# Delta rule of an RWKV-7 layer on Trainium2: one gram product a head, u and v stacked, a bank of its own for the solving

## What is computed

```
sa = einsum('bhvk,bhk->bhv', S, kk_t)
S  = S * w_t[:, :, None, :] - sa[..., None] * b_t[:, :, None, :] + v_t[..., None] * k_t[:, :, None, :]
y_t = einsum('bhvk,bhk->bhv', S, r_t)
```

## Time and profile before

| what | value |
| --- | --- |
| median of 3 runs | 1472.24 us (1471.99 to 1473.29) |
| the profiled execution | 1476.32 us, of which the profile's span is 1474.5 us |
| mean granted PE clock | 0.972 |
| PE busy | 1351.4 us of the span (92%) |
| DVE busy | 783.9 us (53%) |
| ACT busy, POOL busy | 578.9 us (39%), 224.0 us (15%) |
| DMA | 178.46 MB in 249079 packets, of which 151343 are under 512 B |

### The profile page before, as it was taken

How to read it: one execution, slowest core, us unless ns; L and a number is a source line. 1 busy time by engine, 2 the same in 40 slices (tenths; PEclk the granted TensorE clock), 3 DMA queues, 4 the chain that set the end, 5 groups by cost and what they waited for, 6 DMA issues and landing times. The chain is left out here.

```text
span 1474.5 us, 37647 instructions
## 1 busy us (share of the span) xinstructions
PE 1351.4 (92%) x16154; PEld 1215.1 (82%) x16154; DVE 783.9 (53%) x1588; ACT 578.9 (39%) x1178; POOL 224.0 (15%) x335
## 2 busy tenths in 40 slices
PE   7999999999999888777878869999999999998997
PEld 6989898887899887776777748899999997665785
DVE  6737245777831257867777754561111122776545
ACT  6726246876831022222222242441111132876324
POOL 0000000000000255545544700000001000214000
PEclk9999999999999689999999989999999999999998
DMA  5724122567595344455446345024334236431202
GB/s 206 225 60 100 63 89 90 150 180 233 167 262 171 81 95 95 101 116 132 110 99 137 82 163 217 29 84 147 95 91 120 63 110 180 149 102 35 88 29 93
DMA packets 249079, 178.46 MB, mean 121 GB/s; under 512 B 151343, under 2 KB 220911, under 8 KB 247999
## 3 DMA queue, kind: packets, MB, share of 16 engines
q1 hardware_dynamic: 216951, 161.10, 38.5%
q10 hardware_dynamic: 31968, 15.04, 3.6%
HBM read 115.95 MB, written 60.46 MB: 120 GB/s over the span
## 5 line engine op out<-in xcount | busy, mean ns | idle before, releaser
L369 PE MATMUL mix_acc<-mix_high,mix_w_high 128*128 128x364 f32 (+1 forms) x768 | 177.8, 340 | 11.2 <-ACT mix_high L435 10.0
L369 PE MATMUL mix_acc<-mix_low,mix_w_high 128*128 128x364 f32 (+1 forms) x768 | 172.0, 332 | 1.2 <-DVE mix_low L589 1.2
L369 PE MATMUL mix_acc<-mix_high,mix_w_low 128*128 128x364 f32 (+1 forms) x768 | 170.9, 331 | 0.0
L369 PEld LDWEIGHTS mix_acc<-mix_high,mix_w_high 128*128 128x128 f32 x768 | 130.1, 189 | 30.3 <-issue 28.5
L369 PEld LDWEIGHTS mix_acc<-mix_low,mix_w_high 128*128 128x128 f32 x768 | 132.9, 189 | 2.3 <-DVE mix_low L589 2.1
L369 PEld LDWEIGHTS mix_acc<-mix_high,mix_w_low 128*128 128x128 f32 x768 | 133.5, 189 | 0.2 <-DVE mix_w_low L603 0.2
L1579 PE MATMUL out_acc<-qkvg_room_r_high,qkvg_room_w_high 128*128 128x364 f32 (+1 forms) x320 | 105.8, 331 | 1.0 <-DVE qkvg_room_w_low L1931 1.0
L603 DVE TENSOR_TENSOR mix_w_low<-mix_wt,mix_w_high 128x1024 fp32r<-128x1024 f32 x32 | 39.2, 1224 | 124.9 <-ACT mix_w_high L441 124.5
L1579 PE MATMUL out_acc<-qkvg_room_r_low,qkvg_room_w_high 128*128 128x364 f32 (+1 forms) x320 | 105.1, 329 | 0.0
L1579 PE MATMUL out_acc<-qkvg_room_r_high,qkvg_room_w_low 128*128 128x364 f32 (+1 forms) x320 | 105.1, 328 | 0.0
L1929 DVE CAST qkvg_room_w_high<-qkvg_room_wt 128x1024 fp32r<-128x1024 f32 x20 | 14.2, 710 | 155.4 <-DMA qkvg_room_wt<-in_w_att 155.4
(11 more groups left out here) (284 smaller groups left out, 3220.5 us busy)
## 6 DMA issues: line engine op xcount, KB each, us to landing
mix_wt<-in_w_in SPq DMA_DIRECT2D x32, 512.0 KB, 4.6
qkvg_room_wt<-in_w_att SPq DMA_DIRECT2D x20, 512.0 KB, 3.8
delta_bk<-scr_bk SPq DMA_DIRECT2D x17, 512.0 KB, 4.8
delta_kr<-scr_kr SPq DMA_DIRECT2D x17, 512.0 KB, 7.8
scr_kr<-mix_outs SPq DMA_DIRECT2D x16, 512.0 KB, 3.9
scr_bk<-mix_outs SPq DMA_DIRECT2D x16, 512.0 KB, 4.7
early_xpad<-in_xpad SPq DMA_DIRECT2D x8, 548.5 KB, 8.6
scr_xg<-early_xs SPq DMA_DIRECT2D x8, 544.0 KB, 3.0
```

The source lines that it names most:

```text
L369: mm = pe.matmul(acc[:, s, k, 0:width], w[:, s, d, :], r[:, d, n0:n0 + width], start=d == 0 and q == 0, stop=d == DT - 1 and q == 2)
```

## The change

- **Grams**: `bk` is stored as (pair, side, 64), with the two sides exchanged for head 1. One product of a head takes both sides as 128 columns of weights: rows of 64, columns of 128. Bank `gram`p now holds head p, with b's gram on the head's own half and k's on the other. The signs of the masks go by head.
- **u and v stacked**: `uv` holds for each pair and head u on the head's own half and v on the other. `end_y` and the state's update (`make_s`) each contract over all 128 partitions in one product of a head, rows of 128 and columns of 64; the value products of y and of the state are gone. `begin_z` still takes v alone. ACT copies u in two halves (`keep_u`).
- **Rows**: `turn_rows` sends head p to bank `gram`p, both sides, each a quarter; there are as many products as before.
- **Banks**: the solving gets a bank of its own, `solve`; both halves of a level's two products share `level0` and `level1`; the state's update and the turned y use `state_out`.
- ACT copies b's gram to a plain tile `lower` (`keep_lower`, two operations of 64 partitions), from which POOL takes the diagonal blocks and the levels' masks.
- **Order**: `make_grams(front, 0)` comes ahead of `make_u(behind)`; y is turned and gated one turn later; `begin_z` runs beside `make_lm(i, 0)`; `spread_blocks` comes ahead of `make_lm(i, 2)`, `end_z` ahead of `grow(i, 2)`. DVE masks the second half of the grams ahead of the centring, and solves columns 0 to 3 ahead of `scale_y`.
- **Transfers**: `bk` comes in four transfers a chunk (one before), v straight into `uv` in pieces of 64 floats (2 KB rows before).

The core of the diff:

```diff
+def load_pair_of_keys(sp, bk, loaded, scr, slot, t, cols):
+    for p, half in enumerate((slice(0, 64), slice(64, 128))):
+        for k in range(2):
+            sp.dma_start(bk[half, slot, :, k ^ p, :], scr["bk"][t, half, k, :, cols]).then_inc(loaded, 16)
...
-                    for p, f in zip(HALVES, FLIPPED):
-                        sp.dma_start(v_rows[f, c % 3], scr["vt"][c, p]).then_inc(v_loaded[c % 3], 16)
+                    for p in range(2):
+                        sp.dma_start(uv[FLIPPED[p], c % 3, :, p, :], scr["vt"][c, HALVES[p]]).then_inc(v_loaded[c % 3], 16)
...
+                        for p, half in enumerate(HALVES):
+                            mm = pe.matmul(gram_bank[p][:, 128 * j:128 * j + 128], bk[half, c % 2, pair].rearrange("p k n -> p (k n)"), kr[half, c % 4, :, pair, :], start=True, stop=True)
...
+                        for p, half in enumerate(HALVES):
+                            unit = end_diag[half, pair, :] if c < SAMPLE else unit64[half, :]
+                            for side, out_half in enumerate(HALVES):
+                                mm = pe.matmul(gram_bank[p][out_half, 64 * pair:64 * pair + 64], bk[half, slot, pair, side, :], unit, start=True, stop=True)
...
+                def make_s(c):
+                    pe.wait_ge(u_kept, 2 * c + 2)
+                    for p in range(2):
+                        pe.wait_ge(rows_kept[p], c + 1)
+                    if c:
+                        pe.wait_ge(y_gated, c)
+                    for pair in range(DT):
+                        for p, half in enumerate(HALVES):
+                            mm = pe.matmul(state_bank[half, 64 * pair:64 * pair + 64], rows[:, c % 2, pair, p, :], uv[:, c % 3, pair, p, :], start=True, stop=True)
...
+                            mm = pe.matmul(wide_bank[half, 64 * pair:64 * pair + 64], grams[:, c % 3, pair, p, 1, :], uv[:, c % 3, pair, p, :],
+                                           start=False, stop=True, skip_group_check=True)
...
+                def keep_lower(c):
+                    for p, half in enumerate(HALVES):
+                        act.wait_ge(gram_kept[p], 2 * c + 2)
+                        act.activation(lower[half], grams[half, c % 3, :, p, 0, :], ACT.Copy).then_inc(lower_kept, 1)
```

More of the change, by code:

```diff
@@ L1072, in _ @@
                         pool.tensor_tensor(s_sample[:, pair], s_sample[:, pair], end, ALU.mult).then_inc(own_ended, 1)
+                    if front < SAMPLE:
+                        mask_level(front, 0)
+                        mask_level(front, 1)
+                    if 0 <= i < SAMPLE:
+                        end_state(i)
+                    if live(i):
+                        shift_bonus(i)
+                    if front == SAMPLE:
+                        pool.wait_ge(v_sample_loaded, 32)
+                        for b in range(NB):
+                            own = seq_mask[:, b:b + 1].rearrange("p (j n) -> p j n", j=1).broadcast_to([128, DT, 64])
+                            pool.tensor_tensor(v_own[:, b], v_sample[:], own, ALU.mult).then_inc(v_owned, 1)
             @block.tensor
@@ L1171, in end_z @@
+                def end_z(c):
+                    if c:
+                        pe.wait_ge(s_kept, c)
+                    else:
+                        pe.wait_ge(zeroed, 3)
                     pe.wait_ge(z_begun, c + 1)
                     for pair in range(DT):
-                        for p in HALVES:
-                            o = chain_bank[p, 64 * pair:64 * pair + 64]
+                        for half in HALVES:
+                            o = chain_bank[half, 64 * pair:64 * pair + 64]
@@ L1282, in _ @@
                     if live(behind):
[L1283 removed]
+                        begin_y(behind)
                         end_y(behind)
[L1285 to L1290 removed]
                     if live(front):
@@ L1295, in _ @@
                     if 0 <= i < SAMPLE:
+                        wait_for_values(i)
+                        make_lm(i, 0, lambda pair: begin_z(i, pair))
+                        grow(i, 0)
+                    if 0 <= behind < SAMPLE:
+                        make_s(behind)
+                    if live(front):
+                        turn_rows(front)
+                    if 0 <= i < SAMPLE:
                         make_lm(i, 1)
@@ L1298, in _ @@
                     if live(front):
-                        turn_rows(front)
+                        spread_blocks(front)
                     if i == -1:
@@ L1557, in _ @@
                     if live(front):
-                        mask_grams(front, 1, 1)
+                        sum_blocks(front)
                     if 0 <= behind < SAMPLE:
@@ L1563, in _ @@
                     if live(front):
-                        sum_blocks(front)
+                        solve_columns(front, range(4))
                     if 0 <= behind < SAMPLE:
@@ L1568, in _ @@
                         add_grown(i, 2)
-                    if 0 <= behind < SAMPLE:
-                        gate_y(behind)
-                    if live(front):
-                        solve_columns(front, range(4))
 def three_passes(pe, out, w_high, w_low, r_high, r_low, columns):
@@ L2515, in constants @@
     seq = tok[:, None] // NT == tok[None, :] // NT
-    gram = np.stack([np.stack([sign * (m & part)[:, 0:64] for sign, m in ((-1.0, before), (-1.0, upto), (1.0, before), (1.0, upto))], 1)
-                     for part in (np.ones_like(seq), seq)], 1)
+    signs = [np.where(head == p, -1.0, 1.0)[:, None] for p in range(2)]
+    gram = np.stack([np.stack([sign * (m & part)[:, 0:64] for sign in signs for m in (before, upto)], 1) for part in (np.ones_like(seq), seq)], 1)
     col = np.arange(64)
```

350 lines of the change are left out of this document (163 added, 187 removed).

## The result

The changed kernel takes 1459.31 us, the median of four runs (1456.65 to 1461.29), beside 1472.76 us (1471.99 to 1473.55, four runs) for the kernel before. The ratio is 0.9897, with a 95% interval of 0.9867 to 0.9928: faster by 13.4 us (10.6 to 19.6 by the interval), where 32 were forecast. The time lies inside the range of 1418 to 1470; the forecast saving is 2.4 times the measured one and lies outside the interval.

What follows compares the result with a forecast made beforehand. PE, held up by late instruction refills and waits, was taken as the bound, with DVE's 16.0 us a turn as floor; 15 x (20.28 - 17.7) = 39, less 7, saves 32 us: 1444 profiled, 1440 median, range 1418 to 1470.

Steps and rivals of the forecast that it cites:

- The gaps: PE pauses inside equal products, read as late instruction refills: 3.3 us a turn, falling to 1.1 with fewer records.
- The rival in which the refills don't ease: Instruction queue bound by other transfers: gaps stay at 2.8 us a turn or more, 1467 us; 15 in 100.
- Side by side and the changes of shape: New product shapes still share the array; nine more shape changes a turn cost 0.1 us each, 0.9 us.
- the slower rival: Gram halves, end_y and make_s not side by side, each 1.95 us for 0.98: 1490 us; 10 in 100.
- the 0.27 end: Upper cost of a shape change on PE, 0.27 us, if a drain hides nothing of the first product; sum 1461.
- waits for ACT and DVE: The other 2.1 us of PE's 20.28 us turn, the mask's 0.6 among them; 0.8 left after the change.
- the part on the new order: Reordering removes the rows' 0.6 us mask wait and hides ACT's copies; new waits at make_lm and make_u.
- edits at nothing: Edits priced at no time: ACT's extra copies (1.8 us at most), SP's extra transfers, v's smaller pieces, POOL's moved queue.
- forecast turn of 17.7 us: Delta-stage turn after the change: 14.9 stages, 0.9 shape changes, 0.8 waits, 1.1 gaps; before, 20.28 us.
- not a matter of the clock: In the delta stage, a granted PE clock of 0.97 taken as upper level nearly all the time; no term given.
- Start and end: Turn 15's late v_own (5 us), last chunk's u copies (1.2) and turn 0's begin_z (1): 7 us lost.
- the last row of the table: Stretch from the copy of z of chunk 16 to the kernel's end: no change forecast, 0 us.

Runs made afterwards that it cites:

- idle_products: The changed kernel plus 48 products a turn in idle quarters of the array, results unread: 1489.9 us, ratio 1.0065 to the kernel before.
- thin_v: The changed kernel leaving out 7 of 8 pairs in the load of v into uv alone: 1464.4 us, ratio 0.9903 to the kernel before.
- after_again: The changed kernel run and profiled a second time, nothing edited: 1460.7 us, ratio 0.9869 to the kernel before.
- both_moves: The changed kernel with POOL's v_own operations spread over turns 7 to 14 and DVE's sum_blocks ahead of add_state and sum_squares: 1455.2 us, ratio 0.9836.
- sums_first: The changed kernel with sum_blocks on DVE ahead of add_state and sum_squares: 1462.0 us, ratio 0.9883 to the kernel before.
- gram_quarters: The changed kernel with each gram product split into two of 64 columns, in four quarters, 16 more products a turn: 1473.1 us, ratio 0.9933.
- thin_before: The kernel before, leaving out 7 of 8 pairs in the loads of bk, kr, v and the gate: 1453.7 us, ratio 0.9798.
- wide_idle: both_moves plus twelve products a turn of 256 columns in idle quarters, results unread: 1456.3 us, ratio 0.9861 to the kernel before.
- thin_after: The changed kernel, leaving out 7 of 8 pairs in the loads of bk, kr, v and the gate: 1448.9 us, ratio 0.9780.

## Why the prediction was right in its sign and wrong in its size

**The gaps, right.** They were read as PE running out of instructions. Packets went from 4.6 to 3.8 a turn, the gaps from 3.3 to 0.7 us (1.1 forecast), and idle_products brings the packets back to 4.6 and the gaps to 2.4. The rival in which the refills don't ease is out. The reason given for keeping 1.1 us, that v's pieces stand in the refills' way, is refuted by thin_v; that loads as a whole delay refills is right, for about half of the gaps.

**Side by side and the changes of shape, right.** 1.08 us for `end_y` and a gram half; the slower rival needed 1.95. A change costs 0.1 us, and 0.08 by the growth of all stages; the gram half's 0.2 is the exception. On these rows the drain that the Trainium skill names ("TensorEngine Tiling (Array Packing)", Key Properties) is not the 0.27 end: 1.08 against 0.98 us shows 0.1 a change. The sum of 1461 that it would have given (1462.5 when 15 x 1.5 us are added to 1440) came near the time by luck.

**What the turn of before consisted of: misread.** Of the 20.28 us, the prediction took 14.9 for the stages and 3.3 for the gaps, called the other 2.1 "waits for ACT and DVE", and let 0.8 of these stand. The view of the waits does not hold 2.1 us. Besides the rows' 0.6 us, PE's only waits in the 14.0 turns of the earlier trace rows that do not end on "issue" are these:

```profile
PE delta_grown L1154 <- ACT delta_lm L1358: 3.3, 8, 0.5
...
PE delta_lm L1142 <- DVE delta_inv L1460: 1.4, 2, 1.1
```

That is 0.3 us a turn. So 0.9 of the 2.1 us were waits; the rest was PE's own stages, which take 15.6 us and not 14.9, and the clock's loss of 0.56. The rows' 0.6 us went as forecast. After the change the plain turns hold 0.7 to 1.1 us of waits, near the 0.8 left for them, and 16.0 to 16.4 us of stages where 14.9 + 0.9 = 15.8 were counted. Their longest wait is mostly the one for `pick`, a chain through four engines that the part on the new order does not name, and which begins with `keep_lower`, one of the "edits at nothing"; `make_lm` and `make_u`, which it does name, hold PE for little.

The forecast turn of 17.7 us is nevertheless close to the 17.39 measured at full clock, because two errors cancel: 1.1 us of gaps and waits together where 1.9 were left, and stages of 16.3 us where 15.8 were counted. That is luck in part.

**The clock: the step that failed.** The prediction said "not a matter of the clock" and read 0.97 as nothing. 0.97 over the stage is 8.4 us in the fifteen turns, 0.56 us a turn. The turn of 20.28 us contains them, and the forecast turn of 17.7 us is built of stages at full clock, so the sum booked them as saved without a word. Measured, a turn at full clock is 17.39 us, a little under 17.7; over all fifteen it is 18.19, and the 0.8 us between them are, but for 0.1, the clock's loss of 10.3 us. So a loss that was thought gone is there, and somewhat greater (10.3, and 13.3 in the second profile, for 8.4). With it kept, the sum would have had 15 x (20.28 - 17.7 - 0.56) = 30 us for the turns, and 31.0 were measured.

**Start and end, mis-sized.** 7 us were forecast, 11.4 measured: v_own's 4.4 us of wait are as said (5), but the clock falls in it, stays down for 6.8 us, and is 0.80 over the last stretch, which takes 7.3 us more where 6 were forecast (3.3 in the second profile, whose wait is 2.5); the start cost 2.4 for 1; and the last row of the table, 1.7 us, had no term.

**Together.** 32 forecast, less 8 for the turns and 4.4 for start and end, are the 19.6 us of the two traces. The last 6.3 us to the medians' 13.4 lie in the choice of execution. That spread hangs on the clock as well: over its four runs the changed kernel went from 1456.7 us at a mean clock of 0.969 to 1461.3 at 0.964, some 9 us for each 0.01; after_again and both_moves have slopes of 11 and 14, and sums_first, whose four runs lie within 3.4 us, of 3.

## What to carry to other kernels

Price a granted clock of 0.97 like any other term: length times the missing share is time in the turn of before, and it is not removed with the waits around it. Where gaps fall inside rows of equal small products, divide the records by the instruction queue's packets; fewer instructions then buy time even if the array's work stays, until the supply is met. When what is left of a turn is called waits, look whether the view of the waits holds that much. When one wait goes and the median doesn't move, compare the mean of the turns at full clock and the sum of all waits: the shortest turn alone showed 0.4 us won where the mean showed nothing.

## What the runs showed of the hardware that was not expected

- A fall to 1.2 GHz in a stage that is otherwise full mostly comes 1 to 4 us behind the start of a gap of PE of 0.7 us or more, and goes on while PE is busy. The falls lasted 3.4 us before and up to 10.2 us in the kernels with the new shapes. Not every gap brings one: between 530 and 845 us the kernel before had 30 gaps on "issue" of 0.7 us or more and five falls, gram_quarters twelve and eleven, thin_before fifteen and one. Not every fall has one: in both_moves, wide_idle, gram_quarters, thin_v and thin_after one fall each comes over 20 us behind the last such gap. What decides whether one comes and how long it lasts is left open.
- How much a kernel loses to the clock does not follow from how much PE waits. Per turn at full clock, both_moves waits 0.96 us and its profile lost 27.2 us, thin_after waits 1.03 us and lost 3.3, gram_quarters waits 1.60 us and lost 32.3. In the two thinned kernels, with q1 at 16%, the loss was 1.8 and 3.3 us. That the transfers have a part in this is a correlation of a few runs; no run separates it.
- PE in these stages takes a refill of instructions of 16.4 KB for about 250 records, and goes through one in 4.7 us (18.19 us over 3.86); this can hold back a kernel of small products whose operands are all there: with the loads thinned to 16% of the DMA engines the kernel before still had 1.75 us of gaps a turn.
